# Ordering the small matmuls of a chunked recurrence by half instead of by pair, on one core

## The chip, the cores and the metric

One core of a Trainium2 chip runs the whole program. The metric is the device time of one execution in microseconds; the median of three runs is given. The profile is of one execution, taken by the hardware profiler.

## The reference

The program is two model blocks after one another: a first block with a gated mixer and an MLP, and a second block of two layers. Each of these layers has three branches; the change lies in the first of them, a linear recurrence with data-dependent decay (RWKV-7), for 1024 tokens and 6 heads of width 64. Cut to what matters:

```python
def rwkv7_branch(z, mu, w0, w_up, a0, a_up, k_k, k_a, r_k, ln_g, ln_b):
    r, k, v, g, wd, ad = split_cols(token_shift_mix(z, mu), RWKV_COLS)
    w = exp(-DECAY_SCALE * sigmoid(w0 + tanh(wd) @ w_up))
    a = sigmoid(a0 + ad @ a_up)
    kk = normalized(k * k_k); k = k * (1 + (a - 1) * k_a)

    def step(state, inp):                    # one token, for each head
        r_t, w_t, k_t, v_t, kk_t, a_t = inp
        sa = einsum('bhvk,bhk->bhv', state, -kk_t)
        state = (state * w_t[:, :, None, :]
                 + sa[..., None] * (kk_t * a_t)[:, :, None, :]
                 + v_t[..., None] * k_t[:, :, None, :])
        return state, einsum('bhvk,bhk->bhv', state, r_t)

    _, y = lax.scan(step, s0, (r, w, k, v, kk, a))
    ...
```

## The kernel before

The function `rwkv` computes this branch in chunks of 64 tokens. It is called once in each of the two layers. The 1024 tokens are 8 tiles of 128 (NT = 8). A tile holds two chunks, which the code calls halves: half 0 on partitions 0 to 63 and half 1 on partitions 64 to 127. `half(c)` gives the partitions `pr` of half c and `po` of the other.

Each engine runs its own program of trips n = 0 to 8. In trip n TensorE prepares and solves tile n and, mixed in between, finishes tile n-1 (`tail(n - 1)`). VectorE and ScalarE prepare tile n+1 at the same time, and GpSimd makes scaled copies (`be`, `ke`, `rf`, `dg`). Trip 0 has no tile behind it, trip 7 has none ahead, and trip 8 is the tail of tile 7 alone.

The order on TensorE in a trip: `turn_low`, `turns` (transposes of the four scaled inputs), `low`, `values(n-1)`, `score(n, 0..1)`, `solved(n-1)`, `score(n, 2)`, `sums(n+1)`, `turn_first`, and then 15 doubling steps k = 0 to 14, which invert a triangular 64x64 matrix for each head and half. Step k makes `make_P(k+1)`, then takes one piece of the tail by `next(rest, None)`, then `make_T(k)`. Between them VectorE masks each P (`take_P`, L2065) and ScalarE copies each T back (`take_T`, L2188, L2190). There are three groups of two heads, so step k+3 needs the result of step k. ScalarE also works off a list of its own, one item behind each `take_T` from k = 3 on: the first exponential (which needs a table load, L2139), three more exponentials (L2143) with `take_r2` (L2163) among them, `take_S` (L2170), and `take_y` (L2177). VectorE's side list holds `exponents`, `keys`, `take_tr` (L2071) and `scaled` (L2041 to L2047), whose products go to the next trip's `turns`.

The pieces of the tail, one for each step: `outputs` at k = 0; `chunks` for heads 0 and 1, 2 and 3, 4 and 5 at k = 1, 2 and 3; nothing at k = 4, 5 and 6; `carry(0)` at k = 7, which moves the 64x64 state of each head over the first chunk; nothing at 8 and 9; `carry(1)` at k = 10.

All these matmuls are f32 and 64x64, on 64 rows and 64 columns of the 128x128 array. The input partitions give the rows that one uses, and the output partitions the columns; so (pr, pr) and (pr, po) are different quarters. Below, (0,1) is the quarter with the rows of half 0 and the columns of half 1. `outputs`, `make_P`, `make_T`, `values` and `solved` have each half on its own quarter, (0,0) and (1,1), in turn. `chunks` and `score` use all four, `carry(c)` uses (c,c) and (c,1-c). The profile has two records for each f32 matmul.

Of the kernel before, what the change touches and what calls it, by code (L numbers as in the profile page):

```python
# [17 lines left out]
P = 128  # L18
# [24 lines left out]
START = 0  # L43
# [1802 lines left out]
HD = 64  # L1846
# [4 lines left out]
RWH = RW // HD  # L1851
# [12 lines left out]
def heads(ap, n=RWH):  # L1864
    return ap.rearrange("p (h c) -> p h c", h=n)
# [28 lines left out]
def rwkv(nc, A, S, l, hT, Z, L, W):  # L1894
# [3 lines left out]
    NG = 3  # L1898
    LV = 5
    with Phase(nc, "rwkv") as ph:  # L1900
        V = rwkv_constants(A, l, L["early"])["views"]
        ident = L["ident"]
# [8 lines left out]
        be, ke, rf, dg = (ph.sb(n, [P, 3, RW]) for n in ("be", "ke", "rf", "dg"))  # L1911
        xT = ph.sb("xT", [P, NG, 4, P])
        mT = ph.sb("mT", [P, 2, RWH, 4, HD])
        Tb = ph.sb("Tb", [P, 2, NG, 2, 2, HD])
        PS = ph.sb("PS", [P, RWH, HD])
        wv, uw = ph.sb("wv", [P, 3, RWH, P]), ph.sb("uw", [P, RWH, P])
# [3 lines left out]
        bk = ph.ps("bk", [P, 8, 512])  # L1920
        first_in, const_in, in_ = L["rw_first"], L["rw_const"], L["rw_in"]
        step = ph.sem("step")
        names = ("wd_turned wdT_ready lowrank pre sig cums cums_out ex_ready fn_ready f_ready x4_ready "
                 "r6_ready ext_ready turned xT_ready scores masked TT_first T_turned p_made p_out t_made t_out "
                 "dv_made dv_ready uw_made uw_ready last_made tr_ready r2_ready S_made S_ready y_read zeroed").split()
        (wd_turned, wdT_ready, lowrank, pre, sig, cums, cums_out, ex_ready, fn_ready, f_ready, x4_ready,
         r6_ready, ext_ready, turned, xT_ready, scores, masked, TT_first, T_turned, p_made, p_out, t_made, t_out,
         dv_made, dv_ready, uw_made, uw_ready, last_made, tr_ready, r2_ready, S_made, S_ready, y_read, zeroed) = (ph.sem(n) for n in names)
        stored = [ph.sem(f"stored{b}") for b in range(4)]
        N_FIRST, N_CONST = 6, 6  # L1930
        K = NG * LV
# [1 line left out]
        half = lambda c: (slice(64 * c, 64 * c + 64), slice(64 * (1 - c), 64 * (1 - c) + 64))  # L1933
# [3 lines left out]
        both = (slice(0, 64), slice(64, 128))  # L1937
# [3 lines left out]
        with ph.block() as block:  # L1941
# [295 lines left out]
            def _(pe):  # L2237
# [27 lines left out]
                            mm = pe.transpose(bk[:, q, m * P:(m + 1) * P], x4[:, m, q * P:(q + 1) * P], ident[:, :])  # L2265
                        mm.then_inc(turned, 1)

                def score(n, g):
                    banks = ((3, 0), (1, 2), (3, 0))[g]
                    if g < 2:  # L2270
                        pe.wait_ge(xT_ready, START + NG * n + (1, 3)[g])
                    else:
                        pe.wait_ge(masked, START + RWH * n + 2)
                    for q in range(2):
                        for po in both:
                            for pr, bank in zip(both, banks):
                                mm = pe.matmul(bk[po, bank, q * P:(q + 1) * P], xT[pr, g, 2 + q, po], xT[pr, g, 0:2, po], start=True, stop=True)
                                if q and po is both[1]:
                                    mm.then_inc(scores, 1)

                def turn_first(n, g):
                    pe.wait_ge(TT_first, START + NG * n + g + 1)
# [60 lines left out]
                        for pr in both:  # L2343
                            pe.matmul(bk[pr, 7, col(h)], mT[pr, n % 2, h, 3, :], v[pr, h, :], start=False, stop=False, skip_group_check=True)

                def chunks(n, hs):
                    v = heads(part(n, 2))
                    for h in hs:
                        at = col(h)
                        for pr, po in (half(0), half(1)):  # L2350
                            pe.matmul(bk[pr, 4, at], uw[pr, h, HD:P], mT[pr, n % 2, h, 1, :], start=True, stop=False)
                            pe.matmul(bk[po, 6, at], be[pr, n % 3, at], uw[pr, h, 0:HD], start=h == 0, stop=False, skip_group_check=True)
                        for pr, po in (half(0), half(1)):
                            pe.matmul(bk[pr, 4, at], rf[pr, n % 3, at], ident[pr, pr], start=False, stop=True)
                            pe.matmul(bk[po, 6, at], ke[pr, n % 3, at], v[pr, h, :], start=False, stop=False, skip_group_check=True)
                        for pr, po in (half(0), half(1)):
                            mm = pe.matmul(bk[pr, 5, at], uw[pr, h, HD:P], be[pr, n % 3, at], start=True, stop=True)
                    if hs[-1] == RWH - 1:
                        mm.then_inc(last_made, 1)

                def carry(n, c):
                    pr, po = half(c)
                    if c == 0:
                        pe.wait_ge(r2_ready, START + n + 1)
                        pe.wait_ge(tr_ready, START + n + 1)
                    if n or c:
                        pe.wait_ge(S_ready, START + 2 * n + c)
                    for h in range(RWH):
                        pe.matmul(bk[pr, 7, col(h)], r2[pr, col(h)], St[pr, col(h)], start=False, stop=h == RWH - 1, skip_group_check=True)
                        mm = pe.matmul(bk[po, 6, col(h)], tr[pr, col(h)], St[pr, col(h)], start=False, stop=h == RWH - 1, skip_group_check=True)  # L2370
                    mm.then_inc(S_made, 1)

                def tail(n):
                    outputs(n)
                    yield
                    for hs in ((0, 1), (2, 3), (4, 5)):
                        chunks(n, hs)
                        yield
                    yield
                    yield  # L2380
                    yield
                    carry(n, 0)
                    yield
                    yield
                    yield
                    carry(n, 1)
                    yield
# [6 lines left out]
                for n in range(NT + 1):  # L2394
                    ahead, behind = n + 1 < NT, n >= 1
                    if ahead:
                        turn_low(n + 1)
                    if n < NT:
                        turns(n)
                    if ahead:  # L2400
                        low(n + 1)
                    if behind:
                        values(n - 1)
                    if n < NT:
                        score(n, 0)
                        score(n, 1)
                    if behind:
                        solved(n - 1)
                    if n < NT:
                        score(n, 2)  # L2410
                    if ahead:
                        sums(n + 1)
                    rest = tail(n - 1) if behind else iter(())
                    if n < NT:
                        for g in range(NG):
                            turn_first(n, g)
                        make_P(n, 0)
                        for k in range(K):
                            if k + 1 < K:
                                make_P(n, k + 1)  # L2420
                            next(rest, None)
                            make_T(n, k)
                    for _ in rest:
                        pass
# [1262 lines left out]
```

## Time and profile before

| what | value |
|---|---|
| median of 3 runs | 3988.29 us (3980.94 to 3989.87) |
| the profiled execution | 3988.29 us, span 3987.0 us |
| TensorE matmul busy | 3603.1 us, 90% |
| VectorE, ScalarE, GpSimd busy | 2193.1, 1152.0, 479.9 us |
| TensorE's mean granted clock over the span | 0.954 of full |
| the function of the change | from about 2150 to 2412 us and 3405 to 3640 us of the span |

Busy time is the union of an engine's records; a busy TensorE is not TensorE at its peak. In a timeline, each line gives the start, the time from the first record's start to the last one's end, the engine, the source line, the tiles written and read, and the number of records merged into the line; brackets give the idle time before it and what ended it. L2296 is `make_P`, L2307 and L2309 are `make_T`, L2351 to L2357 `chunks`, L2369 and L2370 `carry`, L2277 `score`.

### The profile page before, as it was taken

What the parts mean: (1) busy time and instruction counts of PE and PEld (TensorE: products, weight loads), DVE (VectorE), ACT (ScalarE), POOL (GpSimd) and SP (SyncE); (2) the same over time, 40 slices, a digit from 0 to 9 for tenths busy, and PEclk for the clock granted to TensorE, in tenths of its full rate; (3) what the DMA queues carried; (4) which work ended last, traced back from release to release, by engine and by line L of the source; (5) the groups of instructions that cost most, each with busy time, mean ns of one, the idle gap of its engine ahead of it and who ended that gap; (6) DMA issues with size and microseconds to landing.
All of it is one profiled execution on the core that took longest, in us unless ns stands there. A gap on an engine that the chain in (4) does not pass through costs nothing. (4 is left out here: it accounts for less than half of the span.)

```text
span 3987.0 us, 58152 instructions
## 1 busy us (share of the span) xinstructions
PE 3603.1 (90%) x22944; PEld 2282.5 (57%) x22944; DVE 2193.1 (55%) x4615; ACT 1152.0 (29%) x2493; POOL 479.9 (12%) x300
## 2 busy tenths in 40 slices
PE   5999859799999997999987887998999988788898
PEld 4555434685478544656655775444655656676344
DVE  3143466446764573588875653342388884664343
ACT  2121155220122011411124555222320114555222
POOL 0010013000110010012211211210002221211110
PEclk7999969899999998999998998999999999999999
DMA  6332232323533452123331204111013341212220
GB/s 218 138 116 87 97 116 80 117 95 148 189 106 106 148 189 83 32 64 89 115 110 52 72 20 161 53 65 57 27 48 100 106 137 36 72 34 103 95 79 22
DMA packets 234284, 377.17 MB, mean 95 GB/s; under 512 B 30742, under 2 KB 163870, under 8 KB 233014
## 3 DMA queue, kind: packets, MB, share of 16 engines
q1 hardware_dynamic: 234030, 373.58, 28.4%
q8 instruction: 184, 3.01, 0.3%
q14 instruction: 70, 0.57, 0.0%
HBM read 290.84 MB, written 69.08 MB: 90 GB/s over the span
## 5 line engine op out<-in xcount | busy, mean ns | idle before, releaser
L3399 PE MATMUL win_acc<-across_room,across_hT 128*128 128x384 f32 (+3 forms) x3072 | 908.4, 456 | 3.7 <-PEq L83 3.7
L3399 PEld LDWEIGHTS win_acc<-across_room,across_hT 128*128 128x128 f32 x3072 | 561.3, 191 | 345.4 <-issue 15.5
L2466 DVE TENSOR_SCALAR_CACHE_REDUCE win_rl<-d_sc,win_mid 128x384 f32<-128x384 f32 (+5 forms) x384 | 363.1, 946 | 41.0 <-DVE win_mid L2474 29.1
L3238 PE MATMUL tail_wo<-tail_w_out,across_room 128*128 128x512 f32 x512 | 229.9, 603 | 9.3 <-issue 9.3
L3460 ACT ACTIVATE d_ot<-win_acc 128x384 f32<-128x384 f32 (+1 forms) x144 | 67.0, 467 | 562.0 <-PE win_acc L3399 562.0
L453 PE MATMUL zin_acc<-zin_wt,across_hT 128*128 128x512 f32 (+2 forms) x640 | 229.2, 513 | 0.0
L3249 PE MATMUL tail_wg<-tail_w_gate,across_room 128*128 128x512 f32 x512 | 225.3, 594 | 1.0 <-DVE across_room L3079 1.0
L453 PEld LDWEIGHTS zin_acc<-zin_wt,across_hT 128*128 128x128 f32 x640 | 119.9, 190 | 98.3 <-issue 88.6
L3238 PEld LDWEIGHTS tail_wo<-tail_w_out,across_room 128*128 128x128 f32 x512 | 97.9, 194 | 128.8 <-issue 128.8
L1690 PE MATMUL mlp_bk<-across_hT,across_room 128*128 128x256 f32 x768 | 171.0, 379 | 0.0
L3249 PEld LDWEIGHTS tail_wg<-tail_w_gate,across_room 128*128 128x128 f32 x512 | 96.5, 191 | 116.5 <-issue 116.5
L1690 PEld LDWEIGHTS mlp_bk<-across_hT,across_room 128*128 128x128 f32 x768 | 145.9, 190 | 19.8
L3331 POOL TENSOR_TENSOR win_zp<-win_zp,d_ot 128x3072 f32<-128x3072 f32 (+1 forms) x8 | 44.8, 5604 | 824.4 <-DMA win_zp<-s_z 824.4
L2309 PE MATMUL rwkv_bk<-rwkv_Tb,rwkv_PS 64*64 64x64 f32 x1920 | 129.3, 221 | 11.1 <-DVE rwkv_PS L2065 7.5
L2307 PE MATMUL rwkv_bk<-rwkv_PS,rwkv_Tb 64*64 64x64 f32 x1536 | 110.7, 224 | 19.6 <-DVE rwkv_PS L2065 18.4
L1690 PE MATMUL mlp_bk<-mlp_tsums,mlp_sums 128*128 128x256 f32 x512 | 117.7, 384 | 9.8 <-DVE across_room L1418 9.3
L2065 DVE TENSOR_TENSOR rwkv_PS<-rwkv_bk,layer_early 128x128 f32<-128x128 f32 x240 | 67.6, 287 | 101.6 <-PE rwkv_bk L2296 100.7
L2296 PE MATMUL rwkv_bk<-rwkv_Tb,rwkv_mT 64*64 64x64 f32 x1920 | 102.2, 222 | 20.8 <-ACT rwkv_Tb L2188 16.1
L1239 PE MATMUL mid_wo<-across_room,mid_yT 128*128 128x512 f32 x256 | 114.1, 600 | 3.5 <-ACT mid_yT L1178 3.5
L1377 POOL TENSOR_TENSOR mlp_t<-mlp_t,mlp_rows 128x1024 f32<-128x1024 f32 x8 | 20.2, 2526 | 790.9 <-ACT mlp_t L1624 790.9
L3543 DVE SCALAR_TENSOR_TENSOR d_sc<-win_rl,d_iw,d_sc 128x512 f32<-128x512 f32 (+3 forms) x140 | 92.1, 658 | 41.9 <-ACT win_rl L3476 29.2
L2188 ACT ACTIVATE rwkv_Tb<-rwkv_bk 128x256 f32<-128x256 f32 x192 | 73.5, 383 | 138.2 <-PE rwkv_bk L2309 137.7
(492 smaller groups left out, 6622.9 us busy)
## 6 DMA issues: line engine op xcount, KB each, us to landing
across_room<-in_w SPq DMA_DIRECT2D x96, 1024.0 KB, 6.9
across_room<-in_w_in SPq DMA_DIRECT2D x18, 1536.0 KB, 8.4
s_z<-d_ot SPq DMA_DIRECT2D x14, 1536.0 KB, 6.5
across_room<-in_w_ada SPq DMA_DIRECT2D x8, 2048.0 KB
across_hT<-s_z SPq DMA_DIRECT2D x16, 832.0 KB, 5.7
win_zp<-d_ot SPq DMA_DIRECT2D x8, 1344.0 KB
front_w<-in_w_ada SPq DMA_DIRECT2D x4, 2048.0 KB, 15.6
zin_wt<-in_w_in SPq DMA_DIRECT2D x4, 2048.0 KB, 9.4
```

The lines of the kernel that those rows point to most:

```text
L453: mm = pe.matmul(z, w, x, start=k == 0, stop=k == KC - 1)
L1239: mm = pe.matmul(wo[:, n % 2, c, :], yT[:, n % 2, q, :], w_out[:, q, c * COL:(c + 1) * COL], start=q == 0, stop=q == KC - 1)
L1690: mm = pe.matmul(out, a[:, k, :], b[:, k, :], start=k == 0, stop=k == KC // 2 - 1)
L2188: act.activation(Tb[:, n % 2, g, :, :, :].rearrange("p a h t -> p (a h t)"), bk[:, 2 + k % 2, 0:4 * HD], ACT.Copy).then_inc(t_out, 1)
L2296: mm = pe.matmul(bk[pr, k % 2, col(h)], mT[pr, n % 2, 2 * g + h, 0, :], T_of(n, 2 * g + h, pr), start=True, stop=True)
L2307: pe.matmul(bk[pr, 2 + k % 2, col(h)], TT_of(n, 2 * g + h, pr), PS[pr, 2 * g + h, :], start=True, stop=True)
L2309: mm = pe.matmul(bk[pr, 2 + k % 2, col(2 + h)], PS[pr, 2 * g + h, :], TT_of(n, 2 * g + h, pr), start=True, stop=True)
L2466: s(dve.tensor_scalar(junk[:, q % 2, 0:L], sc[q][:, :], mid[:, q:q + 1], 0.0, ALU.is_gt, ALU.add, accum_out=cnt[:, q:q + 1]))
L3238: mm = pe.matmul(wo[:, c, :], yT[:, n % 2, q, :], W["out"][:, q, c * COL:(c + 1) * COL], start=q == 0, stop=q == KC - 1)
L3249: mm = pe.matmul(wg[:, c, :], xT[:, n % 2, q, :], W["gate"][:, q, c * COL:(c + 1) * COL], start=q == 0, stop=q == KC - 1)
L3399: mm = pe.matmul(acc[:, u % RING, 0:w], hT[:, k, t * P:(t + 1) * P], wt[:, i % 2, k, 0:w], start=k == 0, stop=k == KC - 1)
L3543: dve.scalar_tensor_tensor(x, y, iw, x, ALU.mult, ALU.add).then_inc(summed, 1)
```

## The change

`chunks(n, hs)` becomes `chunk(n, c, hs)`: one half at a time, three heads for each piece, and within a head the matmuls that use one quarter behind each other. There are four pieces (half 0 twice, half 1 twice) in place of three, at k = 1 to 4, and one of the three empty steps goes, so that both carries stay at k = 7 and 10. Half 1 waits for a new semaphore, `half_made`, which half 0's last matmul raises. `carry` has two loops over the heads in place of one. `score` goes by head in place of by pair of heads, so that a head's four matmuls lie on two quarters and the next head's on the other two. The matmuls themselves, their operands and their PSUM banks stay.

```diff
-                def score(n, g):
-                    banks = ((3, 0), (1, 2), (3, 0))[g]
-                    if g < 2:
-                        pe.wait_ge(xT_ready, START + NG * n + (1, 3)[g])
+                def score(n, h):
+                    pr = slice(64 * (h % 2), 64 * (h % 2) + 64)
+                    bank = (3, 0, 1, 2, 3, 0)[h]
+                    if h < 4:
+                        pe.wait_ge(xT_ready, START + NG * n + (1, 1, 2, 3)[h])
                     else:
-                        pe.wait_ge(masked, START + RWH * n + 2)
+                        pe.wait_ge(masked, START + RWH * n + h - 3)
                     for q in range(2):
                         for po in both:
-                            for pr, bank in zip(both, banks):
-                                mm = pe.matmul(bk[po, bank, q * P:(q + 1) * P], xT[pr, g, 2 + q, po], xT[pr, g, 0:2, po], start=True, stop=True)
-                                if q and po is both[1]:
-                                    mm.then_inc(scores, 1)
+                            mm = pe.matmul(bk[po, bank, q * P:(q + 1) * P], xT[pr, h // 2, 2 + q, po], xT[pr, h // 2, 0:2, po], start=True, stop=True)
+                    mm.then_inc(scores, 1)
...
-                def chunks(n, hs):
+                def chunk(n, c, hs):
+                    pr, po = half(c)
                     v = heads(part(n, 2))
+                    if c == 1 and hs[0] == 0:
+                        pe.wait_ge(half_made, START + n + 1)
                     for h in hs:
                         at = col(h)
-                        for pr, po in (half(0), half(1)):
-                            pe.matmul(bk[pr, 4, at], uw[pr, h, HD:P], mT[pr, n % 2, h, 1, :], start=True, stop=False)
-                            pe.matmul(bk[po, 6, at], be[pr, n % 3, at], uw[pr, h, 0:HD], start=h == 0, stop=False, skip_group_check=True)
-                        for pr, po in (half(0), half(1)):
-                            pe.matmul(bk[pr, 4, at], rf[pr, n % 3, at], ident[pr, pr], start=False, stop=True)
-                            pe.matmul(bk[po, 6, at], ke[pr, n % 3, at], v[pr, h, :], start=False, stop=False, skip_group_check=True)
-                        for pr, po in (half(0), half(1)):
-                            mm = pe.matmul(bk[pr, 5, at], uw[pr, h, HD:P], be[pr, n % 3, at], start=True, stop=True)
+                        W = uw[pr, h, HD:P]
+                        pe.matmul(bk[pr, 4, at], W, mT[pr, n % 2, h, 1, :], start=True, stop=False)
+                        pe.matmul(bk[pr, 4, at], rf[pr, n % 3, at], ident[pr, 64 * c:64 * c + 64], start=False, stop=True)
+                        pe.matmul(bk[pr, 5, at], W, be[pr, n % 3, at], start=True, stop=True)
+                        pe.matmul(bk[po, 6, at], be[pr, n % 3, at], uw[pr, h, 0:HD], start=h == 0, stop=False, skip_group_check=True)
+                        mm = pe.matmul(bk[po, 6, at], ke[pr, n % 3, at], v[pr, h, :], start=False, stop=False, skip_group_check=True)
                     if hs[-1] == RWH - 1:
-                        mm.then_inc(last_made, 1)
+                        mm.then_inc(last_made if c else half_made, 1)
...
                     for h in range(RWH):
                         pe.matmul(bk[pr, 7, col(h)], r2[pr, col(h)], St[pr, col(h)], start=False, stop=h == RWH - 1, skip_group_check=True)
+                    for h in range(RWH):
                         mm = pe.matmul(bk[po, 6, col(h)], tr[pr, col(h)], St[pr, col(h)], start=False, stop=h == RWH - 1, skip_group_check=True)
                     mm.then_inc(S_made, 1)
...
                     outputs(n)
                     yield
-                    for hs in ((0, 1), (2, 3), (4, 5)):
-                        chunks(n, hs)
-                        yield
-                    yield
+                    for c in range(2):
+                        for hs in ((0, 1, 2), (3, 4, 5)):
+                            chunk(n, c, hs)
+                            yield
                     yield
                     yield
                     carry(n, 0)
...
                         score(n, 0)
                         score(n, 1)
+                        score(n, 2)
+                        score(n, 3)
                     if behind:
                         solved(n - 1)
                     if n < NT:
-                        score(n, 2)
+                        score(n, 4)
+                        score(n, 5)
```

## Rows read from the trace of the kernel before

**Rows 1.** The page: busy time, share of the span and instructions of each engine.
```profile
PE 3603.1 (90%) x22944; PEld 2282.5 (57%) x22944; DVE 2193.1 (55%) x4615; ACT 1152.0 (29%) x2493; POOL 479.9 (12%) x300
```
**Rows 2.** Windows: the two calls, and three trips of the first call.
```profile
2150.00:2412.00 262.00, 207.39 (x5544) 178.95 (x5544) 143.94 (x356) 138.35 (x296) 48.28 (x40) 0.95 0.19 54
3405.00:3640.00 235.00, 198.09 (x5468) 174.86 (x5466) 129.96 (x329) 127.11 (x280) 43.68 (x37) 0.97 0.15 41
...
core 0: us, PE busy (x) PEld busy (x) DVE busy (x) ACT busy (x) POOL busy (x), PEclk, DMA share, GB/s
...
2228.45:2257.15 28.70, 24.85 (x697) 21.83 (x693) 17.64 (x44) 17.14 (x37) 6.04 (x6) 1.00 0.37 101
2257.15:2287.23 30.08, 25.15 (x697) 21.98 (x694) 17.65 (x44) 17.14 (x37) 6.05 (x6) 1.00 0.42 97
```
**Rows 3.** What TensorE waited for in trips 1 to 6 (2198 to 2375 us).
```profile
PE rwkv_bk L2296 <- ACT rwkv_Tb L2188: 7.9, 6, 1.3
PE rwkv_bk L2307 <- DVE rwkv_PS L2065: 7.8, 12, 1.1
PE rwkv_bk L2309 <- DVE rwkv_PS L2065: 3.2, 13, 0.4
PE rwkv_bk L2309 <- issue: 2.5, 3, 1.1
```
**Rows 4.** Timeline of TensorE in trip 2: make_T 1, make_P 3, make_T 2, make_T 3.
```profile
2240.93 0.28 PE L2307 MATMUL rwkv_bk<-rwkv_PS,rwkv_Tb 64*64 64x64 f32 x4
...
2241.40 0.33 PE L2296 MATMUL rwkv_bk<-rwkv_Tb,rwkv_mT 64*64 64x64 f32 x5
...
2242.34 0.28 PE L2307 MATMUL rwkv_bk<-rwkv_PS,rwkv_Tb 64*64 64x64 f32 x4
...
2243.74 0.31 PE L2307 MATMUL rwkv_bk<-rwkv_PS,rwkv_Tb 64*64 64x64 f32 x4
...
2244.20 0.43 PE L2296 MATMUL rwkv_bk<-rwkv_Tb,rwkv_mT 64*64 64x64 f32 x8
```
**Rows 5.** Timeline of trip 8: two heads of chunks, their end, and carry.
```profile
2404.24 0.27 PE L2352 MATMUL rwkv_bk<-rwkv_uw,rwkv_be 64*64 64x64 f32 x1
...
2404.59 0.27 PE L2352 MATMUL rwkv_bk<-rwkv_uw,rwkv_be 64*64 64x64 f32 x1
...
2406.33 0.28 PE L2357 MATMUL rwkv_bk<-rwkv_be,rwkv_uw 64*64 64x64 f32 x4
2406.66 0.49 ACT L2163 ACTIVATE rwkv_r<-rwkv_bk 128x384 f32<-128x384 f32 x1 [3.81 <-PE rwkv_bk L2357]
```
**Rows 6.** Timeline of carry(1) in trip 7: its first, ninth and last records.
```profile
2395.34 0.27 PE L2369 MATMUL rwkv_bk<-rwkv_St,rwkv_r 64*64 64x64 f32 x1
...
2395.85 0.22 PE L2369 MATMUL rwkv_bk<-rwkv_St,rwkv_r 64*64 64x64 f32 x1
...
2395.86 0.27 PE L2307 MATMUL rwkv_bk<-rwkv_PS,rwkv_Tb 64*64 64x64 f32 x1
...
2396.03 0.22 PE L2369 MATMUL rwkv_bk<-rwkv_St,rwkv_r 64*64 64x64 f32 x1
```
**Rows 7.** Timeline of ScalarE in trip 2, take_T 3 to take_T 7.
```profile
2244.43 0.38 ACT L2188 ACTIVATE rwkv_Tb<-rwkv_bk 128x256 f32<-128x256 f32 x1 [1.02 <-PE rwkv_bk L2309]
2244.83 1.28 ACT L2139 ACT_TABLE_LOAD   x1
2246.13 0.52 ACT L2139 ACTIVATE rwkv_fn<-rwkv_f 128x384 f32<-128x384 f32 x1
2246.68 0.38 ACT L2188 ACTIVATE rwkv_Tb<-rwkv_bk 128x256 f32<-128x256 f32 x1
...
2249.93 0.38 ACT L2188 ACTIVATE rwkv_Tb<-rwkv_bk 128x256 f32<-128x256 f32 x1 [0.48 <-PE rwkv_bk L2309]
```
**Rows 8.** Timeline of VectorE in trip 2, around scaled().
```profile
2251.08 0.56 DVE L2041 TENSOR_TENSOR rwkv_x<-across_hT,rwkv_f 128x384 f32<-128x384 f32 x1 [1.64 <-ACT rwkv_f L2143]
```
**Rows 9.** Timeline of score and sums in trip 2.
```profile
2232.02 1.04 PE L2277 MATMUL rwkv_bk<-rwkv_xT 64*64 64x128 f32 x30
2232.89 1.36 PE L2330 MATMUL rwkv_bk<-rwkv_wv,rwkv_Tb 64*64 64x128 f32 x21
...
2234.93 0.91 PE L2257 MATMUL rwkv_bk<-rwkv_la,layer_early 128*128 128x384 f32 x2
...
2234.03 0.84 ACT L2127 ACTIVATE rwkv_la<-rwkv_la 128x768 f32<-128x768 f32 x1
```

More of the change, by code:

```diff
@@ L1924, in rwkv @@
                  "r6_ready ext_ready turned xT_ready scores masked TT_first T_turned p_made p_out t_made t_out "
-                 "dv_made dv_ready uw_made uw_ready last_made tr_ready r2_ready S_made S_ready y_read zeroed").split()
+                 "dv_made dv_ready uw_made uw_ready half_made last_made tr_ready r2_ready S_made S_ready y_read zeroed").split()
         (wd_turned, wdT_ready, lowrank, pre, sig, cums, cums_out, ex_ready, fn_ready, f_ready, x4_ready,
          r6_ready, ext_ready, turned, xT_ready, scores, masked, TT_first, T_turned, p_made, p_out, t_made, t_out,
-         dv_made, dv_ready, uw_made, uw_ready, last_made, tr_ready, r2_ready, S_made, S_ready, y_read, zeroed) = (ph.sem(n) for n in names)
+         dv_made, dv_ready, uw_made, uw_ready, half_made, last_made, tr_ready, r2_ready, S_made, S_ready, y_read, zeroed) = (ph.sem(n) for n in names)
         stored = [ph.sem(f"stored{b}") for b in range(4)]
```

## The prediction

> **What bounds the kernel now.** I read five views in this order. The page [rows 1] shows TensorE busy for 90% of the span, so TensorE's order of work is worth following wherever it is changed. The diff touches only the recurrence function, which runs twice; its two stretches [rows 2] last 262 and 235 us, 497 of 3987 us, at nearly the full clock (mean 0.95 and 0.97; 1.00, the 2.4 GHz level, in each steady trip shown). A steady trip takes 28.7 to 30.1 us with 25 us of TensorE, 18 of VectorE, 17 of ScalarE: no engine is full, so the waits decide. The waits of TensorE in six steady trips [rows 3] sum to some 25 us of 177, all in the doubling steps (make_P, make_T): for ScalarE's copies (7.9), VectorE's masks (7.8), and 2.5 us "issue", in which it waited for nothing shown. Last come the timelines of one trip: steps 0 to 3 run on TensorE without a gap [rows 4], and behind step 3 ScalarE sets the pace [rows 7].
>
> The unit I need is how small matmuls share the array. An f32 matmul is two records. A 64x64 one uses one of four tiles, (rows, columns), by the partitions that it reads and writes. make_T's 16 records lie on (0,0) and (1,1), 8 each, and take 2240.93 to 2241.40 [rows 4]: 0.0585 us for each record of a tile. I call that a slot. One head of chunks is 20 records on all four tiles and repeats after 2404.24 to 2404.59, 0.35 us [rows 5], which is 6 slots: the 6 records of the fullest tile, with the other three tiles running beside it. So a tile's own records queue at one a slot, and different tiles overlap.
>
> How far ahead may a tile run? In carry(1), 12 records on (1,1) and 12 on (1,0) alternate from 2395.34 to 2396.03. The next make_T's first record, on the free tile (0,0), starts at 2395.86 [rows 6], with the ninth of twelve: when three records per busy tile still wait. I take this as the reach: issue is in order, and a tile holds one running record and three waiting.
>
> At one place the Trainium skill says otherwise ("TensorE: Matmul & The Clock Gate", Part 3, The mechanism): matmuls start and end strictly in program order. The trace disagrees: the 2395.86 record is later in the program than the 2396.03 one [rows 6]. By that rule chunks would gain the same 6 slots a head, and each carry 10 slots in place of the 4 below, which would put the end near 4018 us.
>
> **The change, part by part.** No matmul is added or removed; the order changes, one wait is added, one idle place in the generator goes.
>
> *chunk in place of chunks.* A head and half has 6 records on (c,c) and 4 on (c,1-c); the other half's two tiles are empty meanwhile. Three heads cost 18 slots, 1.05 us, where two heads of both halves cost 12, 0.70 us. The whole trip pays 72 slots for 36. Steps 1, 2, 3 carried 12 slots each and step 4 none; now 1 to 4 carry 18 each. make_P is 4 slots, make_T 8. So make_T of step 3 ends 3 x 6 = 18 slots later, less 2 that I count back where half 0 gives way to half 1: tile (1,1), idle until then, has finished its part two slots before (0,0) by the reach above. 16 slots, 0.93 us. This passes on in full: ScalarE's take_T of step 3 at 2244.43 had waited for TensorE, and behind it stand the table load and the exponential to 2246.65 [rows 7]. Step 4's new 18 slots are hidden under those: from make_T 3's end, 4+18+8 slots are 1.75 us, plus some 0.25 to ScalarE, 2.0 us, where ScalarE comes free some 2.5 us after it (2246.65 [rows 7] against make_T 3's end at 2244.2 [rows 4]). If that cover were gone it would cost another 0.5 us a trip or more. tr and r2 need last_made, now after step 4's chunk, about 1.9 us later relative to make_T 3; VectorE's tr may wait 0.3 us, in front of a take_P with 0.9 us of room. Bounds: 0.5 to 1.3 us.
>
> *carry with its two loops apart.* The 12 records of (c,c) come first; by the reach, (c,1-c) starts with the ninth: 20 slots alone in place of 12. make_T behind it starts from slot 16 in place of slot 12, and ends 4 slots, 0.23 us, later. Behind carry(0) that is exposed: ScalarE's take_T 7 waited for TensorE (0.48 us) [rows 7], and the last exponential behind it releases VectorE's scaled(), which had waited 1.64 us [rows 8]; its products lead to the next turns. Behind carry(1) VectorE is last, so 0. S_made comes 0.47 us later but ScalarE takes it two steps on. Bounds: from 0 (a reach long enough) to 12 slots, 0.70 us (no overlap).
>
> *score head by head.* A head's 4 matmuls take two tiles, the next head's the other two. Eight records, four per tile, are just what one running and three waiting hold, so heads 0 and 1 overlap as before: 32 records in some 0.9 us [rows 9]. The earlier wait on xT for head 0 and on masked for head 4 were long met. 0; at worst the heads run one after the other: 0.9 us more for four heads and 0.45 for two, less about 0.3 of room before sums, which waits for a sigmoid that ends at 2234.87 [rows 9]: 1.05 us a trip.
>
> *the wait on half_made.* It stands in front of half 1 at step 3. Half 0 ended at step 2, with make_T 2 and make_P 4, 12 slots, between: 0. Queued behind it is everything later on TensorE. In the last trip nothing lies between, and TensorE waits for its own pipeline: from the last L2357 records' start near 2406.4 to ScalarE and VectorE starting at 2406.66, and some 0.1 us to restart [rows 5]: 0.35 us, between 0.2 and 0.6.
>
> *The sum.* Trips 1 to 6: 16 + 4 slots = 1.17 us, x6 = 7.0. Trip 7 has no exponentials, so step 4 is not hidden and neither carry: 16 + 18 + 8 slots = 2.46. Trip 8, the tail alone: 36 slots of chunks, 16 of two carries, and the drain: 3.04 + 0.35 = 3.4. Trip 0 has no tail: 0. Together 12.9 us a layer, 25.7 for two.
>
> *A gain against it.* The "issue" stops come in every second trip, where the dense chunks end [rows 3]: 2.5 us in layer 0 and 2.1 in layer 1. With half the records per us these may vanish or move; the range of that term is 0 to -4.6 us and I take -2.
>
> So +23.7 us. The profiled execution took 3988.29 us, span 3987.0 with 1.3 us around it; it is itself the median of the three runs (3980.94 to 3989.87). 3988.3 + 23.7 = 4012 us.
>
> **The rivals.**
> *A: the heads of score run one after the other* (the reach is shorter for the longer records). 16 trips x 1.05 = 16.8 us more: 4029 us. For it: the reach is seen on 64-column records only. Against: 32 such records on four tiles now run in 0.9 us.
> *B: part of the delay is absorbed.* ScalarE idles 1.0 us before take_T 0 to 3 [rows 7], and VectorE has gaps; if only half of make_T 3's delay came through in trips 1 to 6 (12 x 0.47 = 5.6 us) and 7 (2 x 1.0), none of the carries' there, with trip 8 in full (2 x 3.4) and all of "issue" gone (4.6), the sum is 9.8: 3998 us. Against: what follows take_T 3 on ScalarE has no gap until take_T 7.
> *C, the other side: faster.* If the two halves overlapped across steps, 36 slots in all would be spread over four steps, 9 each in place of 12 over three. make_T 3 would end 9 slots, 0.53 us, earlier, in 12 trips: -6.3 us, 3982. It decides from a reach of more than a step's 28 records. Against: in-order issue stops at three waiting [rows 6].
> *D: nothing.* If one tile alone ran its records in under half a slot, the order would be free: 3988. The slot is the same with two tiles (0.0585) and with four (0.35/6), so it isn't shared between tiles.
>
> **How the numbers follow.** As summed: 0.70. A 0.10, B 0.13, C 0.03, D 0.04. The bounds of the likeliest alone, 0.5 to 1.3 us in 12 trips, 0 to 0.7 per carry, 0 to -4.6 of stops, are about 4003 to 4023. 8 in 10, with parts of A and B: 4001 to 4030. 0.2% is 8 us, about what a measurement of this kernel can tell from no change. Faster 0.03, same 0.05, slower 0.92.
>
> **What the profile after would show.** Right: three-head chunks of 1.05 us in steps 1 to 4, with records on two tiles; steps 1 to 4 of 1.75 us where 1 to 3 had 1.40; ScalarE's wait in front of take_T 1 to 3 up from 1.0 to some 1.4 us and its chain unchanged behind the table load; steady trips of 29.9 to 31.2 us; TensorE records of carry separated, 1.1 to 1.2 us from first to last. Score's 32 records still in 0.9 us. Wrong: trips unchanged although the chunks are longer (something else was last), make_T 4 arriving after ScalarE is free, a score of 1.8 us, or chunks of 0.7 us.

## The result, and the profile after

The changed kernel took 4009.87 us (median of four runs, 4005.19 to 4010.8), the kernel before 3986.83 us beside it (four runs, 3980.94 to 3989.87). The ratio on record is 1.0053, 95% interval 1.0039 to 1.0067; the two medians alone give 1.0058. Three further runs of the changed kernel took 4003.47 to 4005.83 us. The prediction was 4012 us, with 0.92 on slower. The profiled execution after has a span of 4010.6 us, 23.6 more than before; it lies at the upper end of these runs.

The page after, its line of busy times, answers to [rows 1]:

```profile
PE 3645.8 (91%) x22944; PEld 2327.5 (58%) x22944; DVE 2196.4 (55%) x4615; ACT 1152.6 (29%) x2493; POOL 480.2 (12%) x300
```

The same number of matmuls keeps TensorE busy for 42.7 us more, and VectorE and ScalarE do what they did. So more busy TensorE was not more work: the same records overlap less. Not all of it lengthens the program, since a part fills time in which TensorE waited.

Windows of the changed kernel: trip 2 of the first call, from one copy of wdT on ScalarE (L2123) to the next, answers to the two trips of [rows 2].

```profile
2225.90:2255.90 30.00, 27.49 (x693) 24.59 (x693) 17.75 (x44) 17.15 (x38) 6.05 (x5) 1.00 0.35 97
```

TensorE is busy for 27.49 of 30.00 us, against 24.85 of 28.70; the other engines' sums are unchanged. Steady trips, measured so in all:

| | trips 2 to 6, layer 0, us | function, first wdT to last yo, us | last trip, us |
|---|---|---|---|
| before | 28.70 30.07 29.04 29.88 29.04 | 255.1, 254.9 | 12.02, 12.95 |
| after | 30.01 30.00 30.01 30.00 30.02 | 265.6, 265.8 | 16.49, 17.52 |

The function's two calls are 10.5 and 10.9 us longer, 21.4 of the 23.6. Two things are to be seen. The stall-free trip went from 28.70 to 30.00. And before, trips scattered upwards from 28.70; after, none does. The waits of TensorE after, in the same stretch of six trips, against [rows 3]:

```profile
PE rwkv_bk L2306 <- DVE rwkv_PS L2065: 6.5, 6, 1.1
PE rwkv_bk L2308 <- DVE rwkv_PS L2065: 3.1, 12, 0.4
PE rwkv_bk L2295 <- ACT rwkv_Tb L2188: 1.6, 6, 0.3
```

make_P's wait for ScalarE's copy fell from 7.9 to 1.6 us: six times 1.3 before, six times 0.3 now. That is the wait behind the table load, and the new chunk of step 4 fills it, as the prediction had it. The line "issue" is gone, in both layers.

ScalarE's timeline after, trip 2, take_T 0 to 3, the table load with its exponential, take_T 4, and take_T 7; it answers to [rows 7]:

```profile
2237.29 0.39 ACT L2188 ACTIVATE rwkv_Tb<-rwkv_bk 128x256 f32<-128x256 f32 x1 [2.31 <-PE rwkv_bk L2308]
2239.04 0.38 ACT L2188 ACTIVATE rwkv_Tb<-rwkv_bk 128x256 f32<-128x256 f32 x1 [1.36 <-PE rwkv_bk L2308]
2240.79 0.39 ACT L2188 ACTIVATE rwkv_Tb<-rwkv_bk 128x256 f32<-128x256 f32 x1 [1.37 <-PE rwkv_bk L2308]
2242.46 0.38 ACT L2188 ACTIVATE rwkv_Tb<-rwkv_bk 128x256 f32<-128x256 f32 x1 [1.29 <-PE rwkv_bk L2308]
2242.86 1.28 ACT L2139 ACT_TABLE_LOAD   x1
2244.16 0.52 ACT L2139 ACTIVATE rwkv_fn<-rwkv_f 128x384 f32<-128x384 f32 x1
2244.71 0.39 ACT L2188 ACTIVATE rwkv_Tb<-rwkv_bk 128x256 f32<-128x256 f32 x1
...
2248.31 0.38 ACT L2188 ACTIVATE rwkv_Tb<-rwkv_bk 128x256 f32<-128x256 f32 x1 [0.82 <-PE rwkv_bk L2308]
```

From take_T 0 to take_T 3 now takes 5.17 us, where it took 4.21 (2240.22 to 2244.43 in the trace before): +0.96. Behind the exponential take_T 4 follows without a wait: step 4's 18 slots are hidden. take_T 7 waits 0.82 in place of 0.48 us: +0.34. The two sum to 1.30, the whole difference of a steady trip.

TensorE's timeline after, one step of trip 2: the three heads of a chunk, make_T's first record, make_P, and the next chunk.

```profile
2239.06 0.28 PE L2353 MATMUL rwkv_bk<-rwkv_mT,rwkv_uw 64*64 64x64 f32 x2
...
2239.41 0.28 PE L2353 MATMUL rwkv_bk<-rwkv_mT,rwkv_uw 64*64 64x64 f32 x2
...
2239.76 0.28 PE L2353 MATMUL rwkv_bk<-rwkv_mT,rwkv_uw 64*64 64x64 f32 x2
...
2240.00 0.27 PE L2306 MATMUL rwkv_bk<-rwkv_PS,rwkv_Tb 64*64 64x64 f32 x1
...
2240.51 0.22 PE L2295 MATMUL rwkv_bk<-rwkv_Tb,rwkv_mT 64*64 64x64 f32 x1
...
2240.75 0.22 PE L2353 MATMUL rwkv_bk<-rwkv_mT,rwkv_uw 64*64 64x64 f32 x1
```

A head of one half repeats after 0.35 us, as a head of both halves did in [rows 5]: two tiles are fed in the time in which four were. make_T's first record, on the half that the chunk leaves empty, starts at 2240.00, with the last head's fifth record on (0,0) (2239.99). Behind that fifth record three wait: the sixth, and make_T's own first two on (0,0), which stand ahead of this one in the program. That is the reach. The step is 1.69 to 1.75 us, where it was 1.40.

carry(0) in trip 2 after, its first records, the first of the second loop, and make_T behind it:

```profile
2246.54 0.73 PE L2369 MATMUL rwkv_bk<-rwkv_St,rwkv_r 64*64 64x64 f32 x9
2247.06 0.27 PE L2371 MATMUL rwkv_bk<-rwkv_St,rwkv_tr 64*64 64x64 f32 x1
...
2247.58 0.27 PE L2306 MATMUL rwkv_bk<-rwkv_PS,rwkv_Tb 64*64 64x64 f32 x2
```

The second loop starts beside the ninth of the first loop's twelve records, as the prediction's reach says. The Trainium skill ("TensorE: Matmul & The Clock Gate", Part 3, The mechanism) has matmuls start and end strictly in program order. The trace disagrees once more: three records of L2369 start behind this one of L2371, at 2247.11, 2247.17 and 2247.23, though they stand ahead of it in the program.

The last trip, layer 0, after: half 0's last chunk record, half 1's first, r2, the two carries and ScalarE's copies of the state. It answers to [rows 5].

```profile
2409.18 0.22 PE L2357 MATMUL rwkv_bk<-across_hT,rwkv_ke 64*64 64x64 f32 x1
2409.45 0.33 PE L2353 MATMUL rwkv_bk<-rwkv_mT,rwkv_uw 64*64 64x64 f32 x2
...
2411.85 0.49 ACT L2163 ACTIVATE rwkv_r<-rwkv_bk 128x384 f32<-128x384 f32 x1 [6.27 <-PE rwkv_bk L2357]
...
2412.51 0.70 PE L2369 MATMUL rwkv_bk<-rwkv_St,rwkv_r 64*64 64x64 f32 x9 [0.70 <-ACT rwkv_r L2163]
...
2414.01 0.49 ACT L2170 ACTIVATE rwkv_St<-rwkv_bk 64x384 f32<-64x384 f32 x1 [1.67 <-PE rwkv_bk L2371]
...
2414.55 1.22 PE L2369 MATMUL rwkv_bk<-rwkv_St,rwkv_r 64*64 64x64 f32 x9 [0.64 <-ACT rwkv_St L2170]
...
2417.09 0.48 ACT L2170 ACTIVATE rwkv_St<-rwkv_bk 64x384 f32<-64x384 f32 x1 [2.60 <-PE rwkv_bk L2371]
```

ScalarE's wait for the chunks grew from 3.81 to 6.27 us: +2.46. From r2 to the first state is 2.16 us, where it was 1.68 (2406.66 to 2408.34 before): +0.48. From the first state to the second it is 3.08, where it was 1.55: +1.53. The same nine records took 0.70 us in carry(0) and 1.22 in carry(1). The windows of the changed kernel (us, then busy times, then the granted clock, third number from the end) say why; the first four lines are layer 0, the last is layer 1:

```profile
2408.00:2411.00 3.00, 2.94 (x81) 2.81 (x80) 0.00 (x0) 0.00 (x0) 0.00 (x0) 1.00 0.00 0
...
2413.00:2414.00 1.00, 0.91 (x19) 0.77 (x17) 0.00 (x0) 0.00 (x0) 0.00 (x0) 1.00 0.06 16
2414.00:2415.00 1.00, 0.46 (x4) 0.46 (x5) 0.00 (x0) 0.49 (x1) 0.00 (x0) 0.63 0.00 0
2415.00:2416.00 1.00, 1.00 (x16) 1.00 (x15) 0.00 (x0) 0.00 (x0) 0.00 (x0) 0.50 0.00 0
...
3650.50:3653.00 2.50, 2.08 (x23) 1.89 (x22) 0.00 (x0) 0.32 (x1) 0.00 (x0) 0.50 0.02 7
```

The granted clock is 1.00 while the chunks run one half at a time, stays there through carry(0), and falls to 0.50, the 1.2 GHz level, between the carries; in layer 1 it falls before carry(0). In the kernel before the same place stays at 1.00 in layer 0 and is at 0.50 in layer 1 from 3633 us on:

```profile
2409.00:2410.00 1.00, 0.79 (x24) 0.65 (x23) 0.00 (x0) 0.10 (x1) 0.00 (x0) 1.00 0.00 0
...
3633.00:3634.40 1.40, 1.38 (x24) 1.19 (x23) 0.00 (x0) 0.00 (x0) 0.00 (x0) 0.50 0.00 0
```

So the fall is not the change's invention. In layer 0 before, it comes too, but only behind the function's last copy: the mean is 0.99 in 2410 to 2411 us and 0.50 in 2411 to 2412. Nor does the changed order bring it every time. Experiment e10 below has the changed kernel's tail but for one wait. There the clock falls between the carries in layer 0, and in layer 1 it stays full up to the second copy of the state. ScalarE's two copies of the state in layer 1, and a window between them:

```profile
3644.43 0.48 ACT L2170 ACTIVATE rwkv_St<-rwkv_bk 64x384 f32<-64x384 f32 x1 [1.67 <-PE rwkv_bk L2369]
...
3646.49 0.48 ACT L2170 ACTIVATE rwkv_St<-rwkv_bk 64x384 f32<-64x384 f32 x1 [1.58 <-PE rwkv_bk L2369]
...
3645.00:3646.00 1.00, 1.00 (x20) 1.00 (x21) 0.00 (x0) 0.00 (x0) 0.00 (x0) 1.00 0.00 0
```

The step from the first state to the second is 2.06 us there at the full clock, against 3.08 with the clock down. The lower clock costs 1.0 us of it, and the order of carry 0.5 (1.55 before).

### The profile page after: what moved, and what is told of

Read it like the earlier page. It is cut to its first block and busy times, and to the rows that moved or that the text cites. A ratio compares the mean times of both kernels' runs of the same rounds, so it can differ in the third digit from the quotient of the medians.

```text
span 4010.6 us, 58154 instructions
## 1 busy us (share of the span) xinstructions
PE 3645.8 (91%) x22944; PEld 2327.5 (58%) x22944; DVE 2196.4 (55%) x4615; ACT 1152.6 (29%) x2493; POOL 480.2 (12%) x300
## 5 line engine op out<-in xcount | busy, mean ns | idle before, releaser
L1690 PEld LDWEIGHTS mlp_bk<-mlp_tsums,mlp_sums 128*128 128x128 f32 x512 | 98.6, 194 | 24.8 <-issue 11.0
```

Of the source, the lines that this page charges most:

```text
L1690: mm = pe.matmul(out, a[:, k, :], b[:, k, :], start=k == 0, stop=k == KC // 2 - 1)
```

## The experiments

All ratios are to the kernel before, run beside each. Slots are the prediction's, 0.0585 us.

**e1: the chunks alone.** `chunk`, `half_made` and the new generator, with `score` and `carry` as before.

```
-                    for hs in ((0, 1), (2, 3), (4, 5)):
-                        chunks(n, hs)
-                        yield
-                    yield
+                    for c in range(2):
+                        for hs in ((0, 1, 2), (3, 4, 5)):
+                            chunk(n, c, hs)
+                            yield
```

> The chunk part of the change alone (half by half, four pieces, the wait on half_made), with score and carry as before. Theory: the two idle quarters cost 16 slots (0.93 us) in make_T 3 in trips 1 to 6, 34 slots in trip 7, 36 slots and 0.35 us in trip 8, 10 us a layer, 20 for two; the stops marked issue vanish (-4): +16 us over before, steady trips of 29.6 us. Rival (the carry or the heads of score make most of the loss): under +8 us.

Measured: 3995.5 us, 14.6 over before, 1.0033 (1.0019 to 1.0048). A trip, by the windows:

```profile
2279.98:2309.64 29.66, 26.86 (x693) 23.83 (x693) 17.76 (x44) 17.14 (x38) 6.05 (x5) 1.00 0.14 45
```

29.65 to 29.67 us in all twelve trips: +0.97, 16.6 slots where 16 were forecast. No issue stop in either layer.

**e2: the carries alone.**

```
                     for h in range(RWH):
                         pe.matmul(bk[pr, 7, col(h)], r2[pr, col(h)], St[pr, col(h)], ...)
+                    for h in range(RWH):
                         mm = pe.matmul(bk[po, 6, col(h)], tr[pr, col(h)], St[pr, col(h)], ...)
```

> The carry part alone. Theory: 4 to 6 slots behind carry(0) in trips 1 to 6, 8 in trip 7, 16 in trip 8: +5 to +7 us in all, with the stops marked issue still there. Rival (strict program order on TensorE): 10 slots a carry, +12 us or more.

Measured: 3990.19 us, 9.3 over before, 1.0029 (1.0018 to 1.0039): more than the 5 to 7 us expected, less than the rival's 12. A trip without a stall:

```profile
2219.93:2248.96 29.03, 25.41 (x693) 22.51 (x693) 17.66 (x44) 17.15 (x39) 6.05 (x5) 1.00 0.35 100
```

+0.33 us, 5.6 slots where the prediction had 4. The issue stops are still there (1.5 us in layer 0, 2.9 in layer 1). 0.97 and 0.33 give 30.00, the changed kernel's trip: the parts add up, so they sit one behind the other on one chain. The twelve trips make 4.0 us of the 9.3; trip 7 is 0.70 us longer (24.56 against 23.86, layer 0) and trip 8 0.99 (13.01 against 12.02). The rest, some 2 us, was not followed.

**e3: score alone.** Head by head, in the changed kernel's places.

```
                         score(n, 0)
                         score(n, 1)
+                        score(n, 2)
+                        score(n, 3)
                     if behind:
                         solved(n - 1)
                     if n < NT:
-                        score(n, 2)
+                        score(n, 4)
+                        score(n, 5)
```

> The score part alone. Theory: the 32 records of heads 0 to 3 still take 0.9 us, 0 us, within 3 of before. Rival (heads one after the other): 1.05 us in each of 16 trips, +17 us.

Measured: 3980.1 us, 0.9995 (0.9985 to 1.0005); a trip without a stall 28.69 us. Score's order costs nothing, and rival A is out.

**e4: the changed kernel, with the two tiles of a half alternating inside a head**, (c,c) and (c,1-c) in turn, in place of three matmuls on one and then two on the other.

```
-                        (c,c) (c,c) (c,c) (c,1-c) (c,1-c)
+                        (c,c) (c,1-c) (c,c) (c,1-c) (c,c)
```

> The whole change, still half by half, but within a head the matmuls of the two quarters alternate as they did before. Theory: the fullest quarter still has 18 records for three heads, so nothing changes: as the changed kernel within 2 us, +22 over before. Rival (it is the run of matmuls on one quarter that costs): at least half of the loss is gone, +11 or less.

Measured: 4004.07 us, 23.2 over before, 1.0054 (1.0037 to 1.007), trips of 30.00 us. The order within a half makes no difference; that one half stands empty does.

**e5: halves in turn, head by head.** The chunks of before (two heads at steps 1 to 3), but of each head half 0's five matmuls and then half 1's five.

```
-                    for h in hs:
-                        for pr, po in (half(0), half(1)):
+                    for h, c in ((h, c) for h in hs for c in range(2)):
+                        pr, po = half(c)
...
```

> The kernel before, three pieces, but inside a head the changed order: five matmuls of half 0, then five of half 1. No wait on half_made. Theory (a quarter holds one running record and three waiting): the next half's quarters are reached almost in time, 2 slots lost over the three steps, 0.1 us a trip: within 4 us of before. Rival 1 (any run of a half costs its full length): as e6 or worse, +12 us or more.

Measured: 3984.22 us, 4.9 over before, 1.0009 (0.9996 to 1.0022): not to be told from no change. The trips without a stall take 28.95 us (one in each layer; the others scatter upwards). The halves take turns twelve times a trip, and yet only 0.25 us, 4 slots, is lost of the 2.1 us that 36 slots would be. Two slots had been expected. Read by the reach, the tiles' queues hold nearly enough to run on while the other half's matmuls are issued.

**e6: halves in turn, two heads at a time.**

```
-                    for h in hs:
+                    for c, h in ((c, h) for c in range(2) for h in hs):
...
```

> The kernel before, three pieces of two heads, inside a piece half 0 of both heads, then half 1 of both. Theory: make_T 3 ends 16 slots later as in the changed kernel, 0.93 us in trips 1 to 7, and 16 slots in trip 8: steady trips of 29.6 us, +15 us less some 4 for the stops marked issue: +11 us. Rival (a long reach, 6 waiting or more): 5 slots or fewer, +3 us.

Measured: 3994.68 us, 15.3 over before, 1.003 (1.0017 to 1.0043); trips of 29.95 us, +1.25. That is 21 slots, where the reach of three gives 16 (5.3 a step). TensorE's timeline of one step: the first chunk record of half 0, the first two of half 1, make_T's first:

```profile
2241.74 0.28 PE L2352 MATMUL rwkv_bk<-rwkv_mT,rwkv_uw 64*64 64x64 f32 x2
...
2242.23 0.27 PE L2352 MATMUL rwkv_bk<-rwkv_mT,rwkv_uw 64*64 64x64 f32 x1
...
2242.33 0.22 PE L2352 MATMUL rwkv_bk<-rwkv_mT,rwkv_uw 64*64 64x64 f32 x1
...
2242.76 0.27 PE L2307 MATMUL rwkv_bk<-rwkv_PS,rwkv_Tb 64*64 64x64 f32 x1
```

Half 1 starts 0.49 us, 8.4 slots, after half 0, where the reach gives 8. Its first record is then followed after 0.10 us in place of 0.06: a tile that had stood empty loses most of a slot. Carry's second loop begins so too (2247.06, then 2247.16 in the changed kernel). This makes about one of the 1.7 slots a step that the forecast lacks; the rest is open. With e5 it shows that the reach is short: between one head (6 records on the fullest tile) and two (12) the loss goes from 4 slots a trip to 21. That it is three records rests on the starts in the timelines (the ninth of twelve here, in [rows 6] and in carry), and both losses are larger than that count gave.

**e7: outputs moved from step 0 to step 4**, under the table load, chunks as before; outputs' waits stay at step 0, and the load that overwrites its operand waits for y as well.

```
-                    outputs(n)
+                    (its waits)
                     yield
                     for hs in ((0, 1), (2, 3), (4, 5)):
                         chunks(n, hs)
                         yield
+                    outputs(n)
                     yield
```

> The kernel before with outputs moved from step 0 to step 4, under ScalarE's table load and exponential; the load of tile rows waits for y_read too. Theory: make_T 3 ends up to 24 slots (1.40 us) earlier, of which VectorE's list lets 1.0 through, and step 4's 24 slots are hidden: -1.0 us in 12 trips, -12 us. Rival (step 4 isn't hidden, or the list of VectorE or ScalarE is last): within 3 us of before.

Measured: 3968.63 us, 10.7 below before, 0.9962 (0.9947 to 0.9976). The fastest trip, in layer 1, takes 27.74 us, -0.96; the expectation of e9 below still goes by 27.92, a trip with 0.18 us of delay in step 3. It is less than the 24 slots (1.40 us) that left step 0, as take_T 0's wait fell by 0.95 only (2.31 to 1.36); the other steps take what they took before. That step 0 without outputs is set by ScalarE and VectorE is inferred from this.

**e8: the chunks of before in four pieces**, two, one, one and two heads at steps 1 to 4.

```
-                    for hs in ((0, 1), (2, 3), (4, 5)):
+                    for hs in ((0, 1), (2,), (3,), (4, 5)):
                         chunks(n, hs)
                         yield
-                    yield
```

> The kernel before with both halves together and four pieces of 2, 1, 1, 2 heads at steps 1 to 4. Theory: 24 slots instead of 36 in front of make_T 3, 0.70 us less in 12 trips, step 4's 12 slots hidden: steady trips of 28.0 us, -8 us. Rival (what stands behind make_T 3 doesn't follow it): within 3 us of before.

Measured: 3965.18 us, 14.2 below before, 0.9955 (0.9938 to 0.9971); trips of 27.98 us, as expected: 12 slots fewer ahead of make_T 3 give 0.72 us. This is the changed kernel's idle place put to use, without the halves apart. The whole gain is larger than the 8 us expected, since the trips hardly scatter: over 27.98 they sum to 1.6 us in both layers, where those of before sum to 6.6 over 28.70. Of the stops that remain, some fall into step 4 and cost nothing there: trip 3 of layer 0 has one of 0.38 us at 2261.51 and takes 27.98.

**e9: both moves, in parts.** Outputs of three heads at step 0 and of three at step 4; chunks of two, one, one and two heads at steps 1 to 4.

```
-                    outputs(n)
+                    outputs(n, (0, 1, 2))
                     yield
-                    for hs in ((0, 1), (2, 3), (4, 5)):
+                    for hs in ((0, 1), (2,), (3,)):
                         chunks(n, hs)
                         yield
+                    outputs(n, (3, 4, 5))
+                    chunks(n, (4, 5))
                     yield
...
```

> The kernel before, with 24 of the 60 slots (of 0.0585 us, one record of a tile) that stand ahead of make_T 3 moved behind it, under the table load: outputs of heads 0 to 2 at step 0 and of heads 3 to 5 at step 4, chunks of two, one, one and two heads at steps 1 to 4. Theory (what stands on TensorE ahead of take_T 3 passes on slot for slot, 24 slots at step 4 are still hidden): a steady trip without a stall of 28.70 - 24 x 0.0585 = 27.30 us, 12 trips -16.8 us, with trip 7 some -19 in all, ratio about 0.9953 or below. Rival (the doubling steps are at the floor that ScalarE and VectorE set, as step 0 was when all of outputs left it: 0.78 us gained of 1.40): 27.6 to 27.9 us a trip, no better than outputs alone or the four pieces alone (27.92, 27.98). Rival (step 4's 24 slots come out from under the table load): take_T 4 waits for TensorE. With the chunks still dense the issue stops should stay, 1 to 4 us a layer; if they go, density isn't their cause.

Measured: 3958.08 us, 24.0 below before, 0.9944 (0.993 to 0.9958), the fastest of all. Two trips by the windows, trip 1 of layer 1 and trip 4 of layer 0, and ScalarE's copies of steps 0, 1 and 2 in the timeline:

```profile
3402.43:3429.73 27.30, 24.76 (x693) 21.86 (x693) 17.76 (x44) 17.15 (x39) 6.08 (x5) 1.00 0.13 42
2272.55:2299.97 27.42, 24.70 (x693) 21.81 (x693) 17.76 (x44) 17.25 (x39) 6.05 (x5) 1.00 0.15 49
```

```profile
2227.96 0.38 ACT L2188 ACTIVATE rwkv_Tb<-rwkv_bk 128x256 f32<-128x256 f32 x1 [1.61 <-PE rwkv_bk L2309]
2229.36 0.38 ACT L2188 ACTIVATE rwkv_Tb<-rwkv_bk 128x256 f32<-128x256 f32 x1 [1.02 <-PE rwkv_bk L2309]
2230.41 0.38 ACT L2188 ACTIVATE rwkv_Tb<-rwkv_bk 128x256 f32<-128x256 f32 x1 [0.67 <-PE rwkv_bk L2309]
```

27.30 us is the expected trip, 1.40 less: slot for slot. The other has 0.12 us of delay spread over steps 3 to 7. Step 0 gave 12 slots' worth in full (2.31 to 1.61), and one head fewer takes 0.35 us off the step from 1.40 to 1.05. The issue stops stay (2.3 us in layer 0, 1.7 in layer 1). Twelve trips make 16.8 of the 24.0 us, and the expectation had some 19 in all; where the rest comes from was not followed.

**e10: the changed kernel without the wait on half_made.**

> The changed kernel without the wait on half_made. The wait's price is then the difference in the last trip alone, where half 1 stands directly behind half 0. Theory (the wait costs the drain of half 0 and the three records of reach): in trip 8 the first half-1 chunk starts 0.2 to 0.4 us earlier than in the changed kernel, where it started 0.27 us after the start of half 0's last records; steady trips stay 30.00 us, since half 0 had long ended there; under 1 us in the whole, not to be told in the time. Rival (the wait also costs in steady trips): trips below 29.9 us. The granted clock in the two carries of trip 8 should again be seen falling, as the stretch ahead of them still feeds one half at a time.

Measured, in one run: 4005.24 us, steady trips of 30.00 us as with it, no issue stops. In the last trip ScalarE's wait for the chunks is 5.79 us where it was 6.27. The wait costs 0.48 us there, and nothing in the steady trips. The clock falls between the carries in layer 0 and not in layer 1, as shown above; the expectation had it falling again, without a word on layers.

## Why the prediction held, and where it did not

The forecast's sum and the trace's, for both layers, in us:

| term | forecast | measured | from |
|---|---|---|---|
| steady trips, 12 | +14.0 | +15.6 | 28.70 to 30.00 |
| trip 7 | +4.9 | +4.7 | 23.86 to 26.21, layer 0 |
| trip 8 at full clock | +6.8 | +6.8 | +2.46, +0.48 and +0.47 each |
| trip 8, clock | none | +2.6 | 1.06 and 2.09 after, less 0.59 before |
| issue stops | -2 | -8.3 | counted below |
| the rest of the program | none | +2.2 | 23.6 less 21.4 |
| sum | +23.7 | +23.6 | |

*The chunks in steady trips* held at 0.96 against 0.93 us: the slot, the reach, the empty half, and the cover of the table load for step 4 (take_T 4 follows the exponential without a wait). e1 shows it alone, e4 that the order within a half plays no part.

*carry(0)* was mis-sized: 4 slots, 0.23 us; it took 0.34 in the changed kernel and 0.33 in e2. make_T starts 1.04 us after carry's first record (2246.54 to 2247.58), 17.8 slots where the prediction had 16. The reach is right (the ninth record). What the count lacked are first records on tiles that had stood empty: the second is 0.05 us later than it would be on a busy tile. Both orders have one such start at carry's beginning. The changed order has two more, where the second loop starts (2247.06) and where make_T starts on (0,0) (2247.58), which by then had stood empty. Before, make_T followed carry on (0,0) without a gap: its first record on the empty tile (1,1) started beside carry's eleventh, its first on (0,0) behind the twelfth.

```profile
2249.14 0.27 PE L2307 MATMUL rwkv_bk<-rwkv_PS,rwkv_Tb 64*64 64x64 f32 x1
...
2249.25 0.22 PE L2307 MATMUL rwkv_bk<-rwkv_PS,rwkv_Tb 64*64 64x64 f32 x2
```

Four slots and twice 0.05 us are 0.33, as measured. Over 12 trips the 0.11 us a trip are the larger part of the 1.6 us.

*carry(1) and score at nothing* held: trips sum to the two terms above, and e3 is at 0.9995.

*Trip 7* came out near, but by two errors that offset each other: the chunks cost 1.68 us (25.54 in e1 against 23.86) where 34 slots are 1.99, and the two carries 0.67 to 0.70 (e2) where 8 slots are 0.47.

*half_made* at nothing in steady trips held (e10). In trip 8 it costs 0.48 us where 0.35 was said, within the 0.2 to 0.6 given; the chunks and the wait together came to 2.46 us against 36 slots and 0.35, 2.45, so the chunks alone are 1.98 where 36 slots are 2.11.

*Trip 8* failed in one step: the slot was taken at the full clock throughout. Around the carries TensorE's granted clock fell to its lower level, 0.50, and the same nine records took 1.22 us in place of 0.70. This is not a fixed price of the new order: in e10 only one of the two layers pays it. No row of the prediction looked at layer 1's last trip, where the trace before already had the fall.

*The issue stops* failed in size. The prediction took -2 of at most -4.6, by the rows named "issue". All of them went. And they had cost more than those rows: trips 1 to 6 of layer 0 sum to 4.2 us over six stall-free ones, where the rows show 2.5; in layer 1 the excess is 2.4 us in these trips, 1.3 in trip 7 (25.20 against 23.86) and 0.35 in trip 8, where the rows show 2.1. Together 8.3. The rows undercount, because a row counts the time in which no record runs, and the last record before a stop still runs for 0.22 to 0.28 us of it. A short stop has no row at all. Trip 6 of layer 0 is 0.34 us too long and has no "issue"; the end of make_T in its step 1 and in its step 2 shows where it went:

```profile
2358.97 0.28 PE L2309 MATMUL rwkv_bk<-rwkv_Tb,rwkv_PS 64*64 64x64 f32 x4
...
2360.37 0.60 PE L2309 MATMUL rwkv_bk<-rwkv_Tb,rwkv_PS 64*64 64x64 f32 x3
```

Four records take 0.28 us from the first start to the last end in step 1; in step 2 three take 0.60.

What causes the stops is not settled. Where both halves ran side by side through whole chunks they were there (before, e2, e3, e5, e7, e8, e9); with chunks of three heads of one half they were gone (after, e1, e4, e10), and e6, between the two, had a row of 0.3 us in layer 0 and none in layer 1, while three of its twelve trips are still 0.4 to 0.5 us longer than 29.95. e2 and e3 have stops too, so neither the carries nor score apart removes them. Among the runs that have them the cost does not follow density simply: 1.6 us in e8 and 5.7 in e9, which issues the same pieces of chunks (trips 1 to 6 of both layers over the stall-free trip). A supply of instructions that dense records outrun would fit, but no run measured the supply.

So the total is nearer than its parts, and that is luck: the stops missed by -6.3 us, the clock by +2.6, the steady trips by +1.6, and 2.2 came from outside the function, which was not followed and is within the scatter of runs. They cancel to 0.1. The mechanism, one half's tiles standing empty ahead of take_T 3, is right by e1 and not by luck.

*The rivals.* A is out by e3. B had the time at 3998 from partial absorption; nothing of the chunks' delay was absorbed in the steady trips, though all of the stops' gain that it counted came. Its "1.0 us before take_T 0 to 3" holds for 1 to 3; take_T 0 had waited 2.31 us. C asked for a reach of 28 records; it is three waiting. D asked for one tile to run its records in under half a slot; a head of one half takes the same 0.35 us as one of both.

## What to carry to other kernels

Small matmuls on different tiles of the array overlapped only as far as a few records here: one running and three waiting on the fullest tile. An order that leaves a row half without work for longer than that adds to every step that another engine waits for; turns of one head (6 records) cost 0.25 us a trip, a fifth to a quarter of what turns of two or three cost (1.25 and 0.97). Count the work that stands on TensorE ahead of the step that another engine waits for, in records of the fullest tile, and move what isn't needed yet under a stretch in which that engine is busy with itself: 24 slots moved from steps 0 to 3 gave all of their 1.40 us a trip (e9), and the same number from step 0 alone 0.96 (e7).

## What was not expected of the hardware

TensorE's granted clock fell to 0.50 in a tail of 24-record bursts between ScalarE's copies, after 3 us at 98% busy on one half at the full clock and waits of 0.6 to 0.7 us. Inside the tail it fell in one layer of two before and in e10, and in both in the changed kernel's trace; in the other layers it fell right behind. It cost 1.0 us for each carry of the changed order run at the lower level. What decides the moment was not tried.

Issue stops of 0.2 to 1.3 us by their rows appear on TensorE where both halves are fed side by side, and none is left where chunks go three heads of one half at a time, with 58,000 instructions in either case. The last record's 0.22 to 0.28 us hide the start of a stop, so that short ones show only in the trips.

A tile that has stood empty runs its first record 0.10 us ahead of the second, in place of 0.06 (2247.06 and 2247.16 in carry's second loop). Two such starts more in a chain are what made carry(0) cost 0.34 us and not 0.23.
